# A four-layer mixed-attention block: three head-projection loops are software-pipelined over four PSUM banks instead of two

## The reference, cut to what matters

```python
def rmsnorm(x, g):
    y = x32 * lax.rsqrt(jnp.mean(x32 * x32, axis=-1, keepdims=True) + EPS)
    return (y * g)

# MLA: 4 heads, q and k have 64 columns without and 32 with rotation
q  = (rmsnorm(c_q, cq_g) @ w_uq).reshape(B, S, 4, 96)
kv = (rmsnorm(c_kv, ckv_g) @ w_ukv).reshape(B, S, 4, 128)
k_nope, v = kv[..., :64], kv[..., 64:]
k = jnp.concatenate([k_nope, broadcast(k_rope over heads)], axis=-1)
q, k = rmsnorm(q, qn_g), rmsnorm(k, kn_g)
q = concatenate([q[..., :64], apply_rope(q[..., 64:], cos, sin)], -1)   # k alike
# NSA: q of 4 heads, k_slc and k_win of one head each; fox: q and k of 4 heads
q, ks, kw = rmsnorm(to_heads(q), qn_g), rmsnorm(k_slc, kn_g[1]), rmsnorm(k_win, kn_g[2])
```

## Time and profile before

| What | Value |
|---|---|
| four runs, median (lowest to highest) | 14535.21 us (14491.75 to 14566.79) |
| the profiled execution, its own time | 14523.37 us |
| span of its slowest core (core 4), the one shown | 14521.8 us |
| spans of the eight cores | 14395.0 to 14521.8 us |
| TensorE, VectorE, ScalarE, GpSimd busy | 67%, 37%, 33%, 6% |

### The profile page before, as it was taken

The page is one execution under the profiler, slowest core; times in us unless marked ns, Lnnn a source line. Parts: engine busy times, 40 slices in busy tenths (PEclk is TensorE's granted clock), DMA queues, the critical chain, the costliest instruction groups (busy, mean ns, idle before and its releaser), DMA issues.

```text
span 14521.8 us, 172333 instructions; the slowest of 8 cores (14395.0 to 14521.8 us)
## 1 busy us (share of the span) xinstructions
PE 9720.0 (67%) x36196; PEld 3700.6 (25%) x36768; DVE 5370.9 (37%) x10993; ACT 4833.6 (33%) x13172; POOL 883.6 (6%) x908
## 2 busy tenths in 40 slices
PE   4934676786682577769677357776958634867696
PEld 1212232232221223223222121322322212133232
DVE  1154532254225453225412445323541244532244
ACT  3533234222453334321254323432125432342212
POOL 0000001200000000220000000031000000003100
PEclk8556567898655656879755565687875556577687
DMA  1001002421000100332100010042210001004211
GB/s 43 3 3 11 6 6 55 76 33 25 10 4 3 12 6 6 72 59 38 20 9 4 3 12 6 6 88 51 33 17 10 3 3 12 6 5 88 50 30 43
DMA packets 537810, 352.77 MB, mean 24 GB/s; under 512 B 281784, under 2 KB 513848, under 8 KB 536800
## 3 DMA queue, kind: packets, MB, share of 16 engines
q0 software_dynamic: 353920, 159.48, 9.4%
q1 hardware_dynamic: 182880, 182.22, 4.3%
...
## 4 chain that ended last, share of the span: by engine, by line
PE 55%; DVE 17%; DMA 9%; issue 9%; ACT 8%; DVEq 1%; ACTq 0%; POOL 0%; another core or an unknown queue 0%; SPq 0%; POOLq 0%
PE pp_ps L374 53%; DMA sb_W<-w_in 4%; DVE sb_tmpF L391 3%; DVE sb_tmpE L409 3%; DMA sb_W<-w_branch 2%; DVE sb_tmpF L409 2%; ACT sb_hT L511 1%; ACT sb_junk L491 1%; ACT sb_stat L388 1%; ACT sb_PT L388 1%; PE pp_psb L374 1%; DVE sb_stgB L391 1%; ACT sb_junk L431 1%; PE pp_ps L379 1%; DVE sb_hT L395 1%
## 5 line engine op out<-in xcount | busy, mean ns | idle before, releaser
L374 PE MATMUL pp_ps<-sb_hT,sb_W 128*128 128x512 bf16 x8880 | 2269.2, 410 | 482.4 <-DMA sb_W<-w_branch 336.3
L374 PE MATMUL pp_ps<-sb_R 64*128 64x512 bf16 (+9 forms) x4224 | 1892.7, 500 | 177.8 <-DVE sb_yst L391 129.7
L379 PE MATMUL pp_ps<-sb_ident,sb_stgB 128*128 128x128 bf16 (+2 forms) x2688 | 475.9, 275 | 1851.6 <-DVE sb_stgB L395 996.3
L388 ACT ACTIVATE sb_PT<-pp_ps 128x512 bf16<-128x512 f32 (+4 forms) x2144 | 1024.4, 483 | 1950.3 <-PE pp_ps L374 1880.8
L388 ACT ACTIVATE sb_tmpE<-pp_ps 128x512 f32<-128x512 f32 (+3 forms) x1168 | 674.8, 578 | 2589.0 <-PE pp_ps L374 2535.5
L374 PE MATMUL pp_ps<-sb_PT,sb_R 128*128 128x512 bf16 (+7 forms) x2604 | 1237.1, 478 | 384.5 <-DVE sb_yst L391 290.8
L374 PE MATMUL pp_ps<-sb_W,sb_R 128*128 128x512 bf16 (+1 forms) x5148 | 1303.5, 397 | 161.8 <-DMA sb_W<-w_o 112.7
L374 PEld LDWEIGHTS pp_ps<-sb_hT,sb_W 128*128 128x128 bf16 x9088 | 908.2, 103 | 1780.5 <-issue 1133.0
L374 PE MATMUL pp_ps<-sb_W,sb_hT 128*128 128x512 bf16 (+4 forms) x4548 | 888.8, 344 | 233.5 <-DMA yT_scr<-sb_yst 76.8
L391 DVE TENSOR_TENSOR sb_x<-pp_ps,sb_x 128x512 f32<-128x512 f32 x1152 | 795.8, 691 | 590.2 <-PE pp_ps L374 585.1
L409 DVE RECIPROCAL sb_tmpE<-pp_ps 64x512 f32<-64x512 f32 x192 | 645.0, 3359 | 766.5 <-PE pp_ps L374 763.6
...
## 6 DMA issues: line engine op xcount, KB each, us to landing
sb_XB<-yT_scr SPq DMA_DIRECT2D x512, 256.0 KB, 3.3
...
sb_W<-w_branch POOLq DMA_DIRECT2D x128, 64.0 KB, 2.9
...
```

What stands on the lines that cost most here:

```text
L374: P.op("pe", lambda e: e.matmul(out, lhsT=lhsT, rhs=rhs, start=start, stop=stop, skip_group_check=True), R, W)
L379: P.op("pe", lambda e: e.matmul(out, lhsT=in_, rhs=idt[0:k, 0:k], start=True, stop=True, skip_group_check=True), R, W)
L388: P.op("act", lambda e: e.activation(out=out, in_=in_, func=func, **kw), R, W)
```

## The change

`proj_T` is taught to run stage B as a Python generator, which gives way at marked places. Without `lock`, a tile's generator runs to its end once two later tiles have had their stage A (before: one). With `lock`, the generators wait until four are active, and then the two oldest run in turns, one marked piece of each. All passes named above but the rope-key pass take four PSUM banks (0, 1, 5, 6); scratch, staging tiles and statistics columns are doubled and their keys carry the tile's parity. In mkv the square sum moves from VectorE to ScalarE: 64 columns are squared per head there, and the part of the 32 shared rope columns comes from `krb`, made once per layer in the rope-key pass. The diff, cut: doubled scratch names in `nsa_cons` and `fox_cons` and the `yield` lines in them are left out where they only repeat.

```diff
-        kfull = sb("kfull", [128, 2, 96], F32)
+        kfull2 = sb("kfull", [128, 2, 2, 96], F32)
+        krb = sb("krb", [128, 16], F32)
...
-        def proj_T(wsrc_list, ncols, consumer, lhs_fn=None, nk=8, psel=(0, 1)):
+        def proj_T(wsrc_list, ncols, consumer, lhs_fn=None, nk=8, psel=(0, 1), lock=False):
...
+            active = []
...
                 nxt = consumer(it, ps[:, 0:ncols], ("ps", pi))
-                if pend is not None:
-                    pend()
-                pend = nxt
+                if nxt is not None and not hasattr(nxt, "__next__"):
+                    if pend is not None:
+                        pend()
+                    pend = nxt
+                    continue
+                if nxt is not None:
+                    active.append(nxt)
+                if lock and len(active) == 4:
+                    two, active = active[:2], active[2:]
+                    while two:
+                        for g_ in list(two):
+                            try:
+                                next(g_)
+                            except StopIteration:
+                                two.remove(g_)
+                while not lock and len(active) > 2:
+                    for _ in active.pop(0):
+                        pass
...
             def mla_kr_cons(it, ps, pk):
                 CP("act", krope[:, it, :], ps, [pk], [("krope", it)])
+                P.op("act", lambda e, it=it: e.activation(out=junk[:, 0:32], in_=ps, func=AF.Square,
+                                                        accum_out=krb[:, it:it + 1]), [pk], ["krb"])
+                TS("dve", krb[:, it:it + 1], krb[:, it:it + 1], 1.0 / 96.0, EPS, ALU.mult, ALU.add, ["krb"], ["krb"])
...
-                def rope_and_T(qn, it, dstbuf, pr, nm):
+                def rope_and_T(qn, qnk, it, dstbuf, pr, nm):
+                    par = it % 2
+                    pb = par * 512
...
+                    rk_ = ("tmpFc", par)
...
+                    sgk = ("stgB", nm, par)
...
+                    yield
                     for hh in range(2):
...
                 def mq_cons(it, ps, pk, pr=pr):
...
-                        TT("dve", qn, sq, bc(gb[:, 0:96].unsqueeze(1), [128, 2, 96]), ALU.mult, ["tmpFa", "gb"], ["tmpFb"])
-                        rope_and_T(qn, it, QA, pr, "QA")
-                    return stB
+                        TT("dve", qn, sq, bc(gb[:, 0:96].unsqueeze(1), [128, 2, 96]), ALU.mult, [("tmpFa", par), "gb"],
+                           [("tmpFb", par)])
+                        yield
+                        yield from rope_and_T(qn, ("tmpFb", par), it, QA, pr, "QA")
+                    return stB()
...
+                proj_T([(wsrc, 192)], 192, mq_cons, lhs_fn=lambda kc, it: cqT[:, kc, it * 128:(it + 1) * 128], nk=3, psel=(0, 1, 5, 6), lock=True)
...
                 def mkv_cons(it, ps, pk, pr=pr):
                     kv3 = ps.rearrange("p (h c) -> p h c", h=2)
+                    base = (it % 4) * 16 + 14
+                    skeys = ssq_A([ps[:, 0:64], ps[:, 128:192]], base, [pk])
                     CP("act", VA[:, it, :, 0:64], kv3[:, :, 64:128], [pk], [("VA", it)])
-                    TT("dve", sq, kfull[:, :, :], kfull[:, :, :], ALU.mult, ["kfull"], ["tmpFa"])
-                    RED(ss, sq, ["tmpFa"], [sk])
-                    RSTD(ss, 96.0, sk)
...
+                    ss = stat2[:, base:base + 2]
+                    ACT(ss, ss, AF.Ln, skeys + ["krb"], skeys, bias=krb[:, it:it + 1], scale=1.0 / 96.0)
+                    ACT(ss, ss, AF.Exp, skeys, skeys, scale=-0.5)
+
+                    def stB():
+                        par = it % 2
+                        kfull = kfull2[:, par, :, :]
+                        kfk = ("kfull", par)
+                        CP("dve", kfull[:, :, 0:64], kv3[:, :, 0:64], [pk], [kfk])
+                        CP("dve", kfull[:, :, 64:96], bc(krope[:, it, :].unsqueeze(1), [128, 2, 32]), [("krope", it)], [kfk])
...
+                        yield
+                        yield from rope_and_T(kn, ("tmpFb", par), it, KA, pr, "KA")
+                    return stB()
...
+            proj_T([(wl[:, 1312:1568], 256), (wl[:, 1696:1952], 256)], 512, nsa_cons, psel=(0, 1, 5, 6))
...
+                        (wl[:, 2476 + pr * 128:2476 + (pr + 1) * 128], 128)], 384, fox_cons, psel=(0, 1, 5, 6))
```

More of the change, by code:

```diff
@@ L536, in proj_T @@
                 nxt = consumer(it, ps[:, 0:ncols], ("ps", pi))
-                if pend is not None:
-                    pend()
-                pend = nxt
+                if nxt is not None and not hasattr(nxt, "__next__"):
[16 more added lines that the diff above has]
+                        pass
             if pend is not None:
                 pend()
+            while lock and active:
+                for g_ in list(active):
+                    try:
+                        next(g_)
+                    except StopIteration:
+                        active.remove(g_)
+            for g_ in active:
+                for _ in g_:
+                    pass
         def proj_F(wsegs, m, consumer, psel=(0, 1)):
@@ L763, in rope_and_T @@
                     t2 = qn[:, :, 80:96]
[L764 to L767, removed]
+                    a = tmpF[:, pb + 384:pb + 416].rearrange("p (h c) -> p h c", h=2)
+                    b = tmpF[:, pb + 416:pb + 448].rearrange("p (h c) -> p h c", h=2)
+                    c2 = tmpF[:, pb + 448:pb + 480].rearrange("p (h c) -> p h c", h=2)
+                    d2 = tmpF[:, pb + 480:pb + 512].rearrange("p (h c) -> p h c", h=2)
+                    rk_ = ("tmpFc", par)
                     csb = bc(cs.unsqueeze(1), [128, 2, 16])
                     snb = bc(sn.unsqueeze(1), [128, 2, 16])
[L770 to L775, removed]
-                    CP("dve", sg[:, :, 0:64], qn[:, :, 0:64], ["tmpFb"], [sgk])
-                    TT("dve", sg[:, :, 64:80], a, b, ALU.subtract, ["tmpFc"], [sgk])
-                    TT("dve", sg[:, :, 80:96], c2, d2, ALU.add, ["tmpFc"], [sgk])
+                    TT("dve", a, t1, csb, ALU.mult, [qnk, "cossin"], [rk_])
+                    TT("dve", b, t2, snb, ALU.mult, [qnk, "cossin"], [rk_])
+                    TT("dve", c2, t2, csb, ALU.mult, [qnk, "cossin"], [rk_])
+                    TT("dve", d2, t1, snb, ALU.mult, [qnk, "cossin"], [rk_])
+                    sgb = stgB[0] if nm == "QA" else stgB[1]
+                    sg = sgb[:, par * 256:par * 256 + 192].rearrange("p (h c) -> p h c", h=2)
+                    sgk = ("stgB", nm, par)
+                    CP("dve", sg[:, :, 0:64], qn[:, :, 0:64], [qnk], [sgk])
+                    TT("dve", sg[:, :, 64:80], a, b, ALU.subtract, [rk_], [sgk])
+                    TT("dve", sg[:, :, 80:96], c2, d2, ALU.add, [rk_], [sgk])
+                    yield
                     for hh in range(2):
@@ L817, in layer @@
+                    return stB()
                 wsrc = wukv_d[l][:, pr * 256:(pr + 1) * 256]
-                proj_T([(wsrc, 256)], 256, mkv_cons, lhs_fn=lambda kc, it: ckvT[:, it * 128:(it + 1) * 128], nk=1)
+                proj_T([(wsrc, 256)], 256, mkv_cons, lhs_fn=lambda kc, it: ckvT[:, it * 128:(it + 1) * 128], nk=1, psel=(0, 1, 5, 6), lock=True)
                 if pr == 0:
```

86 lines of the change are left out of this document (50 added, 36 removed).

## The result

The changed kernel takes 14020.61 us (median of 11 runs, 13883.31 to 14295.52) against 14538.69 for the kernel before (16 runs, 14478.0 to 14645.86): a ratio of 0.9604, interval 0.957 to 0.9639. 14060 was forecast. The profiled execution took 13945.11 us; its slowest core, core 1, spans 13943.6 and is the one shown. Runs in which one die ran at a lower granted clock are left out of every ratio.

A forecast was written before the change was run, and what follows sets the result against it. Waits, not a full engine, were taken to bound the mkv passes, a serial chain per tile. Terms -357 - 16 - 72 - 45 + 15 = -475 took 14523 to 14048, 14060 us on the median's footing; range 13960 to 14190.

The forecast's parts named there:

- mkv: Eight MLA key/value passes: two VectorE instructions a tile go, two tiles are woven; 3.36 us a tile, -357 us.
- Rival 2: MLA query and key/value passes: VectorE's spacing does not shrink; +16 + 15 on the forecast, 14091 us; chance 0.09.
- The cover: MLA passes: VectorE's work on one pair hides 4.9 us of copies and the next two tiles' statistics.
- the third rival: MLA's 16 passes: pairs do not overlap, VectorE idles 4.9 us in each of 128; +152, 14687 us; chance 0.03.
- mq: Eight MLA query passes: the same weaving, no instruction removed; one wait of 0.12 us goes per tile, -16 us.
- The rule that was cited against it: Trainium skill: VectorE's flush comes with or without a semaphore; mq would gain nothing, mkv 2 us a pass less.
- NSA: Four NSA passes: four banks let TensorE run two tiles ahead, ScalarE becomes the bound; 18 us a pass, -72 us.
- Only when the bank is free: NSA passes before: TensorE's next eight matmuls start only once the bank is free; ScalarE waits 3.11 us for TensorE.
- fear of the clock: NSA and fox: TensorE's clock eats the gains, NSA saves 32 in all, fox nothing; 14145 us; chance 0.14.
- The expected clock above 0.85: Changed NSA passes: TensorE's granted clock would be above 0.85, where it was 0.77.
- fox: Eight fox passes: 2.66 us of ScalarE per tile, 47.9 us a pass against 53.5; -45 us.
- Rope-key: Four rope-key passes: a ScalarE square and VectorE scale added per tile, each square awaiting the scale; 0.70 us, +15 us.

The follow-up runs named there:

- pairs_two_banks: Changed kernel with mq and mkv on two PSUM banks, each pair finished before the next starts: mkv 570.77 us, mq 545.51; ratio 0.9736 to the kernel before.
- no_weave: Changed kernel without `lock=True` in mq and mkv, so tiles are not woven, four banks kept: mkv 459.86 us, mq 383.13; no ratio.
- own_keys: Changed kernel with separate keys for rotation scratch, staging parts and kfull halves in mq and mkv: mkv 280.51 us, mq 267.59; ratio 0.9368 to the kernel before.
- banks_by_layer: Changed kernel with NSA and fox on two, four, three, four banks by layer, stage B one tile behind in layers 1-2, two in 3-4: 14310.86 us.

## Why the prediction was right, point by point

The mechanisms held where they carried most of the sum, but every term was sized too small, the gains and the rope-key pass's cost alike: -532 in the windows for -475.

**mkv (-357, was -376).** The step held: VectorE alone bounds the pass, covered by the lead. A tile takes 3.22 and not 3.36, because an instruction that needs no fresh result starts 0.08 before the end of the one ahead, not 0.02: the gain to the next 0.28 instead of 0.34, the last add to the next 0.11 instead of 0.17 (843.25 to 843.66 for the two, which start 0.30 apart). Lead-in 1.68, forecast 1.75. Rival 2 erred to the other side.

**The cover** was named rightly and priced wrongly: 2.1 to 2.9 us per pair, not 4.9, because the serial sum counted statistics that run beside VectorE's first half. So the third rival could not have come out slower: with 322 us instead of 627 it stands at -532 + 322 = -210, and pairs_two_banks is faster than the kernel before.

**mq (-16, was -26).** The same mis-sized wait: 0.20 a tile (26 us over 128 tiles), not 0.12. The mechanism is the weave, shown by no_weave. The rule that was cited against it does not hold for these chains, as own_keys shows.

**NSA (-72, was -94).** The bound was right (ScalarE, 3.50 a tile: 56 us and 6 for the ends), the reason half wrong. "Only when the bank is free" named the last semaphore; banks_by_layer shows that the order of TensorE's queue held the group more than the bank did. The change altered both, so the number came out, in this part by luck. The value taken was below the upper bound for fear of the clock; 23.6 of the possible 24.9 a pass came. The expected clock above 0.85 came in two of four passes and changed nothing.

**fox (-45, was -55).** 16 x 2.67 as forecast, with ends of 3.8 us and not 5.3. The gain is the order, with the third bank that it needs: four banks in the old order gave nothing. Some 9 of the 55 us are two passes of the kernel before that ran at granted clocks of 0.83 and 0.82 and took 56.4 and 57.6 us, where the other six took 51.7 to 53.7.

**Rope-key (+15, was +19).** 0.70 a tile as worked out. The missing 4 us are the ends: 16 x 0.70 leaves out 1.1 us a pass, which the 7.5 that it was set against contains. And the chain of rows was only the last of several bounds: without it the tile takes 0.62, and with reads of one bank set free some 0.5 (9.2 less 1.1 for the ends, over 16).

**The rest.** -46 stands in stages that did not change, whose length goes with their granted clock on every core; it is no part of the prediction.
